# x's first rows and the first norm weight loaded by halves around the first weight chunks, the first half split ahead of the first chunk, and eight idle products on TensorE

## The reference

```python
def rmsnorm(x, g):
    xf = x.astype(jnp.float32)
    y = xf * lax.rsqrt(jnp.mean(xf * xf, axis=-1, keepdims=True) + EPS)
    return (y * g.astype(jnp.float32)).astype(x.dtype)

def swiglu(x, w_gate, w_up, w_down):
    return (jax.nn.silu(x @ w_gate) * (x @ w_up)) @ w_down

    # first_block, first line of its loop
    x = x + 0.5 * swiglu(rmsnorm(x, ff1_norm[l]), ff1_w_gate[l], ff1_w_up[l], ff1_w_down[l])
```

## Time and profile before

| what | value |
|---|---|
| device time, median of 3 runs | 1291.72 us (1291.45 to 1293.63) |
| the profiled execution's own time | 1292.1 us |
| its span, first to last instruction | 1290.4 us |
| PE busy | 1261.6 us, 98% of the span |
| DVE, ACT busy | 765.1 us (59%), 608.9 us (47%) |
| first product on PE starts at | 7.27 us |
| from this point on PE runs without a wait of the first layer | 15.75 us |
| last product on PE ends at | 1282.96 us |

### The profile page before, as it was taken

How to read it: one execution, slowest core, us unless ns; L and a number is a source line. 1 busy time by engine, 2 the same in 40 slices (tenths; PEclk the granted TensorE clock), 3 DMA queues, 4 the chain that set the end, 5 groups by cost and what they waited for, 6 DMA issues and landing times.

```text
span 1290.4 us, 15419 instructions
## 1 busy us (share of the span) xinstructions
PE 1261.6 (98%) x6000; PEld 1031.3 (80%) x6000; DVE 765.1 (59%) x1027; ACT 608.9 (47%) x807; POOL 49.8 (4%) x111
## 2 busy tenths in 40 slices
PE   7999999999999999999999999999999999999997
PEld 5888887888888888888877657888887888788886
DVE  6755546756665665555455557555556776655554
ACT  6443435456557355454445344444434454444441
POOL 2000002100000000000010011000001000000001
PEclk9999999999999999999999999999999999999999
DMA  8655555754443556655646425755664644655551
GB/s 285 204 179 196 195 165 174 243 178 132 131 128 129 189 179 209 194 180 193 194 104 208 129 95 177 240 174 182 203 191 158 194 149 118 225 193 183 181 190 54
DMA packets 119752, 226.55 MB, mean 176 GB/s; under 512 B 8049, under 2 KB 16241, under 8 KB 119681
## 3 DMA queue, kind: packets, MB, share of 16 engines
q1 hardware_dynamic: 116976, 216.10, 51.9%
q0 software_dynamic: 2560, 8.95, 2.4%
q10 hardware_dynamic: 144, 0.52, 0.1%
HBM read 224.50 MB, written 1.05 MB: 175 GB/s over the span
## 4 chain that ended last, share of the span: by engine, by line
PE 89%; DVE 5%; POOL 2%; DMA 1%; issue 1%; ACT 1%; DVEq 0%; SPq 0%; POOLq 0%; ACTq 0%
PE ps L392 27%; PE ps L395 27%; PE ps L400 27%; PE ps L356 3%; DVE wl L1377 2%; DMA raw<-in_gla_w_in_dram 1%; PE ps L551 1%; PE ps L565 1%; POOL st L2104 1%; DVE X L1459 1%; DMA raw<-in_ff_w_gate_dram 1%; PE ps L704 1%; PE ps L706 1%; DVE XTL L1415 0%; POOL st L2103 0%
## 5 line engine op out<-in xcount | busy, mean ns | idle before, releaser
L1377 DVE TENSOR_TENSOR wl<-raw,wh 128x1024 fp32r<-128x1024 f32 x409 | 487.4, 1219 | 248.9 <-ACT wh L846 246.1
L846 ACT ACTIVATE wh<-raw 128x1024 fp32r<-128x1024 f32 x409 | 422.6, 1054 | 229.6 <-PE ps L400 196.6
L392 PE MATMUL ps<-wh,XTH 128*128 128x512 f32 (+1 forms) x1184 | 453.6, 387 | 1.2 <-ACT XTH L879 1.2
L395 PE MATMUL ps<-wl,XTH 128*128 128x512 f32 (+1 forms) x1184 | 445.6, 380 | 3.5 <-DVE wl L1377 3.5
L400 PE MATMUL ps<-wh,XTL 128*128 128x512 f32 (+1 forms) x1184 | 347.1, 379 | 0.4 <-DVE XTL L1415 0.4
L392 PEld LDWEIGHTS ps<-wh,XTH 128*128 128x128 f32 x1184 | 223.3, 189 | 47.3 <-issue 5.9
L395 PEld LDWEIGHTS ps<-wl,XTH 128*128 128x128 f32 x1184 | 223.3, 189 | 46.6 <-DVE wl L1377 7.0
L400 PEld LDWEIGHTS ps<-wh,XTL 128*128 128x128 f32 x1184 | 215.9, 188 | 44.0 <-DVE XTL L1415 1.6
L392 PE MATMUL ps<-wh,HHf 128*128 128x512 f32 x352 | 137.8, 391 | 0.0
L395 PE MATMUL ps<-wl,HHf 128*128 128x512 f32 x352 | 137.1, 390 | 0.0
L400 PE MATMUL ps<-wh,HLf 128*128 128x512 f32 x352 | 108.4, 389 | 0.0
(11 more groups left out here) (268 smaller groups left out, 986.4 us busy)
## 6 DMA issues: line engine op xcount, KB each, us to landing
raw<-in_ffn_w_gu_dram SPq DMA_DIRECT2D x88, 512.0 KB, 4.6
raw<-in_w_in_dram SPq DMA_DIRECT2D x56, 512.0 KB, 3.8
raw<-in_ff_w_gate_dram SPq DMA_DIRECT2D x44, 512.0 KB, 4.4
raw<-in_ff_w_up_dram SPq DMA_DIRECT2D x44, 512.0 KB, 4.6
raw<-in_ff_w_down_dram SPq DMA_DIRECT2D x44, 512.0 KB, 4.0
raw<-in_ffn_w_down_dram SPq DMA_DIRECT2D x44, 512.0 KB, 4.4
raw<-in_gla_w_in_dram SPq DMA_DIRECT2D x24, 512.0 KB, 4.6
raw<-in_moba_w_in_dram SPq DMA_DIRECT2D x24, 512.0 KB, 4.4
```

What stands on the lines that cost most here:

```text
L392: e.matmul(o, lh[:, kt, rows(t)], wh[:, s, w], start=kt == 0, stop=False)
L395: e.matmul(o, lh[:, kt, rows(t)], wl[:, s, w], start=False, stop=False)
L846: e.activation(wh[:, j % NS, 0:m], raw[:, j % NR, 0:m], ACT.Copy).then_inc(S("wh"), 1)
L1377: e.tensor_tensor(wl[:, j % NS, 0:m], raw[:, j % NR, 0:m], wh[:, j % NS, 0:m].bitcast(F32), ALU.subtract).then_inc(S("wl"), 1)
```

## The change

x's first row tile is loaded in two halves: half 0 ahead of chunk 0, half 1 between the chunks 0 and 1. The norm weight comes in two halves too, both on ACT's queue. Each half has a semaphore of its own. DVE scales half 0 and computes its low part ahead of chunk 0's split; half 1 is scaled after chunk 0's split, and its low part is computed after chunk 1's. ACT copies half 0 into XTH ahead of chunk 0's `wh`, and half 1 after chunk 1's `wh`. PE transposes half 1 only after chunk 0's products. And PE begins with eight products of `ident` with itself into PSUM bank 7, which nothing reads.

```diff
         def sp_program(e):
-            e.dma_start(X[:, 0, :], x[0, 0:P, :]).then_inc(S("x0"), 16)
+            e.dma_start(X[:, 0, cols(0)], x[0, 0:P, cols(0)]).then_inc(S("x00"), 16)
             load_chunk(e, 0)
+            e.dma_start(X[:, 0, cols(1)], x[0, 0:P, cols(1)]).then_inc(S("x01"), 16)
             load_chunk(e, 1)
...
         def pe_first(e, name, stage, halves):
             for now in pe_gemm(e, name, XTH, XTL, wait_x(stage), 4):
+                if now == (0, 1) and stage == 1:
+                    pe_turn_x(e, 1, 0, 1)
...
         def pe_program(e):
+
             e.wait_ge(S("const"), 2)
-            for h in range(2):
-                pe_turn_x(e, 1, 0, h)
+            for _ in range(8):
+                e.matmul(ps[:, 7, 0:P], ident[:, :], ident[:, :], start=True, stop=True)
+            pe_turn_x(e, 1, 0, 0)
...
-                                        squares(r, h, S(f"x{r}"), 16)
+                                        squares(r, h, S("x1" if r else f"x0{h}"), 16)
...
-            e.dma_start(gbc[:, :], ff1_norm[0].partition_broadcast(P)).then_inc(S("gbc_first"), 16)
+            for h in range(2):
+                e.dma_start(gbc[:, cols(h)], ff1_norm[0, cols(h)].partition_broadcast(P)).then_inc(S(f"gbc_first{h}"), 16)
             tables("silu_and_others")
-            high_to(0)
-            for h in range(2):
-                split_x(1, 0, h)
+            split_x(1, 0, 0)
+            high_to(1)
+            split_x(1, 0, 1)
             high_to(3)
...
-            e.wait_ge(S("x0"), 16)
-            e.wait_ge(S("gbc_first"), 16)
-            for h in range(2):
-                scaled_x(0, h)
+            e.wait_ge(S("x00"), 16)
+            e.wait_ge(S("gbc_first0"), 16)
+            scaled_x(0, 0)
+            low_x(1, 0, 0)
             low_to(0)
-            for h in range(2):
-                low_x(1, 0, h)
+            e.wait_ge(S("x01"), 16)
+            e.wait_ge(S("gbc_first1"), 16)
+            scaled_x(0, 1)
             low_to(1)
+            low_x(1, 0, 1)
             e.wait_ge(S("x1"), 16)
```

## The result

The changed kernel took 1297.09 us, median of 11 runs (1294.45 to 1298.76); the kernel before, on the same chip, 1292.33 (1291.05 to 1294.15). The ratio is 1.0033, with a 95% interval of 1.0024 to 1.0042. It is slower by about 0.33%, which is 4.3 us by the ratio and 4.8 by the medians. The prediction was 1291.1, and its range ended at 1293.2. The profiled execution took 1298.72 us for a span of 1297.0, where the one before had 1290.4, so its surplus is 6.6 us.

The account below looks back on a forecast made before the run. PE bounds the kernel, its start set first by chunk 0's landing, then by DVE until 15.71 us. `wl` 2 ready at 15.15, 0.6 earlier, carries through: 1291.72 - 0.6 = 1291.1 us, range 1290.3 to 1293.2.

Parts of the forecast that it names:

- clock up: At the start, idle products raise PE's clock for chunk 0's products; `wl` 2 ready 0.6 us earlier; chance 0.45.
- the argument from the program's end: After the last product the clock fell only after 4.2 us idle, so a rise survives PE's start gaps, under 2 us.
- the landing of the first halves at 5.0: At the start, first halves of x and gbc land at 5.0 us, so SC begins at 5.1 instead of 6.43.
- before DVE asks for it: At the start, ACT copies XTH of half 1 at 11.35 to 11.9, ahead of DVE's XTL at 12.15.
- rival 3: At the start, the halves come no earlier than the whole, SC at 6.43; 1292.7 us, chance 0.03.
- rival 1: At the start, the clock stays down until chunk 0 is through; 1.15 us later, 1292.9 us, chance 0.35.
- clock down: At the start, chunk 0's products run 0.43 apart and DVE's second XTL waits for PE; `wl` 2 1.15 us later.
- this slow level costs nothing, since DVE is the limit until 15.71: At the start of the kernel before, PE's lower clock was claimed to cost nothing, DVE being the limit until 15.71 us.
- Nothing afterwards takes the shift back or adds to it: After the start, later stages and loads move along with PE, so the start's shift passes unchanged to the end.
- Rival 2: At the start, chunk 0 still lands at 8.7 us; +0.7 with the faster clock, 1292.4 us; chance 0.12, both clocks.

Follow-up runs that it names:

- idle_only: The kernel before plus only the eight idle products at PE's start; 1294.55 us, ratio 1.0012.
- idle_p1: The kernel before plus the eight idle products, one single execution; 1294.28 us beside 1291.68 for the kernel before.
- idle_p3: The kernel before plus the eight idle products, a further single execution; 1294.32 us beside 1291.68 for the kernel before.
- idle_p4: The kernel before plus the eight idle products, a further single execution; 1294.16 us beside 1291.68 for the kernel before.
- more_idle: The changed kernel with 12 idle products in place of 8, 6 more behind the first transposes, 4 behind chunk 0's first product; 1295.07 us, ratio 1.0017.
- changed_again: The changed kernel run once more, against the kernel before; 1297.85 us over five runs, ratio 1.0033.
- again: The kernel before, unchanged, as a second sample; 1292.93 us, ratio 0.9999.
- order_only: The kernel before with only the new order of DVE, ACT and PE, whole loads and no idle products; 1295.99 us, ratio 1.0021.
- no_idle: The changed kernel without its eight idle products, sampled twice against the kernel before; 1295.75 us, ratio 1.0022, and 1296.39 us, ratio 1.0024.
- idle_again: The kernel before plus the eight idle products, a second sample; 1294.09 us, ratio 1.0010.
- idle_tiny: The kernel before plus eight idle products of only 2 columns each at PE's start; 1293.86 us, ratio 1.0013.
- loads_only: The kernel before with only x's first tile and gbc loaded in halves, old order, no idle products; 1293.51 us, ratio 1.0000.
- kept_up: The kernel before plus 12, 6 and 2 idle products up to chunk 0, and SC of row tile 1 behind `wl` of chunk 2; 1293.65 us, ratio 0.9999.
- idle_wide: The kernel before plus two idle products of 512 columns each at PE's start; 1292.66 us, ratio 1.0002.

## Why the prediction was wrong

**Failed: the likeliest case, "clock up".** The idle products ran from 1.58 to 5.37, as forecast (3.79 us), but chunk 0's products were still 0.43 apart from 11.60 on. In both profiles of the changed kernel the clock's first rise is at 13.4 and 16.4 us, so the idle products did not raise it at all. In four of the six profiles of the kernel before with the same eight (idle_only, idle_p1, idle_p3, idle_p4) they did, and there the argument from the program's end, that a rise once won is held over 4.2 us of idleness, failed: in idle_p1 the clock was up from 5.4 to 8.8 us and down again from then to 15.7. Its stretches:

```profile
5.50:8.70 3.20, 1.31 (x8) 0.84 (x8) 1.39 (x2) 0.00 (x0) 2.42 (x11) 1.00 0.95 271
9.00:15.00 6.00, 4.57 (x10) 3.38 (x11) 5.17 (x7) 4.83 (x6) 0.00 (x0) 0.50 1.04 409
```

In the first PE is busy 1.31 us of 3.20, and the clock falls behind it.

**Failed: the sum for "clock up", -0.6.** more_idle had that clock and began `wl` 2 at 15.27, where 14.0 stood in the sum: 1.3 more, and 0.71 later than before. The term that was off is the first, the landing of the first halves at 5.0: SC began at 6.28 instead of 5.1 (6.04 in the changed kernel, where the first half of `gbc` landed at 5.94), `wl` 0 at 9.64 instead of 8.3, the second XTL at 13.46 instead of 12.15. The lengths of the steps between were about right, but the overlap was not: the sum had XTH of half 1 ready "before DVE asks for it", and with the head 1.3 late DVE waited 0.68 us for it. The DVE queue's slack of 0.25 us in the sum was all that the new order had. The DMA view of 0 to 1.6 us, changed kernel, last column the time to landing:

```profile
gbc<-in_ff_norm_dram ACTq DMA_DIRECT2D x2, 256.0 KB, 5.9
raw<-in_ff_w_gate_dram SPq DMA_DIRECT2D x1, 512.0 KB, 6.9
X<-in_x_dram SPq DMA_DIRECT2D x1, 256.0 KB, 4.8
```

5.9 is the median of the two halves of `gbc`. x's 256 KB needed 4.8 us, where the whole 512 KB needed 5.4 in the kernel before, and 5.1 in changed_again where again has 5.1 for the whole: here, dividing bytes by the rate of the earlier trace rows did not give the landing of the first load. Chunk 0 landed at 8.13 instead of 7.05, inside the bounds.

**Called least likely, and it came true: rival 3**, "the halves come no earlier than the whole", with a chance of 0.03. Over the six profiles with halved loads SC began at 6.31 in the mean against 6.41 with whole ones. The rival was priced with the clock up only (1292.7), and never together with rival 1, though nothing in the one excludes the other. That is why the range ended too early. Put SC 1.2 us later into the prediction's own sum for "clock down" (1.15), and it gives an estimate of 2.35; the profiles show 1.83 to 2.60.

**Right in its mechanism, too small: rival 1.** Products 0.43 apart, DVE idle before its second XTL (2.03 us), SC and `wl` 2 behind it: that is what happened. Its price was 1.15; it measured +1.85 in the profile. The 0.7 between are again the head, that is rival 3: SC at 6.04 for 5.1, `wl` 0 at 9.52 for 8.7, XTL at 14.52 for 13.9, `wl` 2 from 16.41 for 15.7. In changed_again the rise of the clock came only at 16.4 us (13.4 in the first profile), and it was +2.56; order_only and the two no_idle, with SC at 6.46, 6.26 and 6.33, had +2.4 to 2.6. The ratios of 1.0021 to 1.0024, 2.7 to 3.1 us, agree with these.

**Wrong: "this slow level costs nothing, since DVE is the limit until 15.71".** again shows PE as the limit of the same kernel when chunk 0 lands at 8.06. One profile was read as the kernel.

**Wrong: "Nothing afterwards takes the shift back or adds to it".** With rival 1 at its measured 2.5 us the time would have been 1294.8, so some 2.3 us of the 4.8 between the medians are left for this. The idle products were costed at nothing because they end before SC. Eight of them cost 0.10 to 0.13% in three comparisons (idle_only, idle_again, idle_tiny), each with an interval whose lower end is just at or above none (1.0001, 1.0000, 1.0003), and the difference between the changed kernel and no_idle, 0.11%, says the same. Where a profile shows a loss of weights it is at 680 to 702 us. How the idle products bring it about stays open.

**Held:** the halves by themselves change nothing later (loads_only is 1.0000). Rival 2, chunk 0 still at 8.7, did not occur in the profile of the changed kernel. It would have cost little more: with SC this late, `wh` 0 stands behind XTH of half 0 in ACT's queue and begins at 8.44 to 8.91 in all profiles with the new order, wherever chunk 0 lands.

## What to carry to other kernels

When an engine's in-order queue gets a job that waits on a round trip through other engines, price it by the slowest leg at the slowest clock, and look at what stands behind it: one XTL ahead of `wl` instead of behind it, with its XTH on ACT, cost 1.3 us here (2.60 against 1.26). If two rivals do not exclude each other, price both together: here they came together. Idle products to raise the clock had to reach up to the work (more_idle, kept_up); the eight alone were lost. They also cost 0.1%, and far away from where they stand, so measure them alone; two wide ones did not show that cost, though one comparison is thin ground for a rule. And take a start from two or three executions before calling an engine's slowness free, or a load early.

## What the runs showed of the hardware

- Adding 16 matmul records and 16 weight loads to the head of PE's program went with weights 0.78 to 2.09 us late in a stage 680 us further on, in 7 of 9 profiles; four wide ones, equally long, did not (-0.11; ratios 1.0013 for idle_tiny and 1.0002 for idle_wide).
- The granted clock falls to 0.50 for 3.4 or 6.8 us in the middle of the program, in 16 of 20 profiles, and mostly at the same places: 697 to 699, 800 to 805, 1103 us. One of 3.4 us costs 1.55 to 1.65 us, one of 6.8 us 3.1 to 3.2. Those at 697 to 699 come at 16 products of two columns (1.92 us of them). Ahead of these PE had waited 1.89 to 2.32 us for LA in the three profiles whose fall lasts 6.8 us (idle_tiny and the two changed ones), and 0.11 to 1.30 in the eight where it lasts 3.4. Those at 800 to 805 and 1103 come about 2 us after a wait of 1.29 to 1.36 us for X; the kernel before waited 1.32 at the same place in the earlier trace rows's execution and had no fall. So what PE does there does not decide alone. The Trainium skill, "TensorE: Matmul & The Clock Gate", section "HAM oscillation — how this bites in real kernels", tells of the clock falling as PE waits for loads. In none of these rows does PE itself wait for a load: it waits for LA or X, or, in idle_wide at 696.5, hardly at all. The stretches of idle_wide:

```profile
696.60:699.80 3.20, 3.20 (x9) 2.49 (x8) 1.26 (x2) 0.40 (x1) 0.00 (x0) 0.50 0.85 272
1102.80:1106.00 3.20, 3.20 (x9) 2.47 (x8) 1.80 (x3) 1.42 (x2) 0.02 (x1) 0.50 0.86 234
```

- A good part of the spread between executions of one kernel (1290.4 to 1294.2 us for the 21 of before beside idle_tiny) goes with the clock: the correlation of span and mean granted clock over those runs is -0.74, and -0.59 to -0.82 in the other sets of before.
- 256 KB in halves landed hardly earlier than the 512 KB as a whole at the very start: the first SC, which waits for `gbc`, at 6.31 in the mean of six profiles against 6.41 in the mean of 14.
